# Merge stage of a two-block network on one core: gated sums by halves of the tokens, low parts on VectorE, last tile by halves of the columns

## Chip, cores and metric

One core of a Trainium2 chip runs the whole program. The metric is the device time of one execution in microseconds (us); a time is the median of several runs. The engines are named as in the profile: PE (TensorE, with PEld for its weight loads), DVE (VectorE), ACT (ScalarE), POOL (GpSimd) and SP (SyncE, which here only issues DMAs).

## What is computed

The program computes two blocks over 1024 tokens of 1024 features: a convolution mixer with a mixture of experts, then a block with sparse attention beside a state-space scan. The change touches the last lines of the second block alone:

```python
g_att, g_ssm = jnp.split(gate_logits, 2, axis=-1)
merged = jax.nn.sigmoid(g_att) * y_att + jax.nn.sigmoid(g_ssm) * y_ssm
x = x + gate[:, None, :] * (merged @ w_out[l])
```

`merged` and `x` are 1024 x 1024, `w_out` is 1024 x 1024, `gate` is one row of 1024.

## The kernel before

The last stage is `merge_out_stage`. What it reads: `k.y_ssm` (the scan's branch, in SBUF, features on the partitions, 8 chunks of 128 features x 1024 tokens, complete when the stage begins), and in DRAM `gates_dram`, whose chunks 0 to 7 hold sigmoid(g_att) * y_att (called att) and whose chunks 8 to 15 hold sigmoid(g_ssm) (called sig), `w_out_2` (the weights) and `x_dram`.

The product is made of float16 pairs: each float32 operand is split into a high part (rounded to float16) and a low part (what is left, in float16), and `product` (lines 140 to 142) issues three matmuls of 128 x 128 by 512 for every 512 columns: high by high, high by low, low by high. Weights are split by `high_part` on ACT (line 407) and `low_part` on DVE (line 412).

The stage has two phases. In the chunk loop over c = 0 to 7 (KC = 8), SP loads three tiles of 512 KB for each chunk, in the order weights, sig, att, each into a ring of four buffers (lines 2839, 2842, 2845). For c of 4 and more each load waits until its buffer is free: weights for `low`, sig for `summed`, att for `m_low`. The order of the work on each engine:

- DVE: the low part of weights 0; then for each c the product sig * y_ssm (line 2902), the sum with att (line 2905), and the low part of the weights of c + 1.
- ACT: the copy of the gate out of PSUM (line 2886); then for each c the high part of the weights (line 407) and the high part of the sums (line 2891).
- POOL: for each c the low part of the sums (line 2919).
- PE: for each c, when the four parts are there, the matmuls of the token tiles 0 to 3 (four tiles x two column halves x three), accumulated in the four PSUM tiles `mg_ps` of 1024 columns, two banks each.

In the second phase PE makes the token tiles 4 to 7, all eight chunks for each tile, 48 matmuls. For each of the eight tiles DVE multiplies the PSUM tile by the gate (line 2913), POOL adds the result to x (line 2924), and SP stores the tile of 512 KB (line 2849). x (4 MB) is loaded behind the last load of the chunk loop (line 2846). A PSUM tile is used again when its product with the gate is done (`gated_done`), a buffer of `gated` (two of them) when POOL's add is done (`added`).

All orders are written out by hand; an engine runs its list in order, and semaphores named above join the lists. What stands ahead of the stage on the engines is the scan's last projection; its last DVE instruction starts at 2716.70 us.

## Time and profile before

| | us |
|---|---|
| median of 3 runs | 2838.12 (2835.35 to 2838.47) |
| the profiled execution, its own time | 2832.92 |
| its span | 2831.1 |
| PE busy | 2513.3 (89%) |
| DVE busy | 1654.6 (58%) |
| ACT busy | 953.8 (34%) |
| POOL busy | 621.5 (22%) |
| the merge stage: first load issued, end of the span | 2718.42, 2831.1 |

The whole profile's shares are averages over stages with different limits; the merge stage is 4% of the span, and it is read by the views of its own stretch. In a row, times in a timeline are the start and the duration in us; a duration in a group of rows is the mean in ns; the last field of a row is the idle time of the engine just before it, with the instruction that ended it. PEclk is the granted clock of TensorE, 1.00 for 2.4 GHz and 0.50 for 1.2 GHz.

### The profile page before, as it was taken

What the parts mean: (1) busy time and instruction counts of PE and PEld (TensorE: products, weight loads), DVE (VectorE), ACT (ScalarE), POOL (GpSimd) and SP (SyncE); (2) the same over time, 40 slices, a digit from 0 to 9 for tenths busy, and PEclk for the clock granted to TensorE, in tenths of its full rate; (3) what the DMA queues carried; (4) which work ended last, traced back from release to release, by engine and by line L of the source; (5) the groups of instructions that cost most, each with busy time, mean ns of one, the idle gap of its engine ahead of it and who ended that gap; (6) DMA issues with size and microseconds to landing.
All of it is one profiled execution on the core that took longest, in us unless ns stands there. A gap on an engine that the chain in (4) does not pass through costs nothing. (4 is left out here: it accounts for less than half of the span.)

```text
span 2831.1 us, 39742 instructions
## 1 busy us (share of the span) xinstructions
PE 2513.3 (89%) x15455; PEld 1351.1 (48%) x15455; DVE 1654.6 (58%) x2909; ACT 953.8 (34%) x1486; POOL 621.5 (22%) x513
## 2 busy tenths in 40 slices
PE   5999594698889998589799979998999999999978
PEld 3555343354445554245334447743454444444433
DVE  5777785332223332576399986643684766746842
ACT  6110503121112222555452225531453534615510
POOL 1012123000000000332342200000450721703613
PEclk8999797799999999799899989999999999999999
DMA  9554878499999998320112210043002002020051
GB/s 240 191 167 132 286 247 318 165 384 388 386 386 372 380 366 316 100 67 23 39 37 82 104 38 1 1 149 127 16 1 97 8 1 97 8 90 8 1 218 80
DMA packets 129230, 433.06 MB, mean 153 GB/s; under 512 B 27760, under 2 KB 37360, under 8 KB 120752
## 3 DMA queue, kind: packets, MB, share of 16 engines
q1 hardware_dynamic: 99872, 365.39, 35.3%
q0 software_dynamic: 10176, 32.78, 3.7%
q10 hardware_dynamic: 19024, 32.67, 3.4%
q8 instruction: 113, 1.85, 0.3%
q14 instruction: 45, 0.37, 0.0%
HBM read 371.86 MB, written 58.94 MB: 152 GB/s over the span
## 5 line engine op out<-in xcount | busy, mean ns | idle before, releaser
L1254 PE MATMUL m_gu<-conv_y,m_xT 128*64 128x256 f32 x1024 | 234.1, 388 | 18.6 <-DMA arena<-in_moe_w_up 16.3
L1256 PE MATMUL m_gu<-arena,m_xT 128*64 128x256 f32 x1024 | 234.1, 388 | 0.0
L2307 POOL TENSOR_TENSOR group_words<-group_words 128x1024 f16<-128x1024 f16 x64 | 149.8, 2361 | 373.7 <-PE i_pj L142 364.5
L1333 DVE TENSOR_TENSOR m_hid<-m_sg,m_gu 64x256 f32<-64x256 f32 x96 | 39.6, 412 | 320.4 <-ACT m_sg L1302 320.4
L1256 PEld LDWEIGHTS m_gu<-arena,m_xT 128*64 128x64 f32 x1024 | 143.3, 140 | 73.9 <-issue 15.4
L1276 PE MATMUL m_y_ps<-arena,m_hidT 128*64 128x512 f32 x768 | 175.4, 598 | 0.0
L1302 ACT ACT_TABLE_LOAD x48 | 61.6, 1283 | 297.5 <-issue 285.0
L1254 PEld LDWEIGHTS m_gu<-conv_y,m_xT 128*64 128x64 f32 x1024 | 143.3, 140 | 36.9 <-issue 26.1
L140 PE MATMUL i_pj<-hT,group_words 128*128 128x512 f16 x384 | 146.5, 382 | 14.7 <-DVE group_words L412 9.3
L140 PE MATMUL s_pj<-hT,arena 128*128 128x512 f16 x384 | 148.7, 387 | 0.0
L141 PE MATMUL s_pj<-hT,arena 128*128 128x512 f16 x384 | 148.5, 387 | 0.0
L142 PE MATMUL s_pj<-hT,arena 128*128 128x512 f16 x384 | 148.1, 386 | 0.0
L141 PE MATMUL i_pj<-hT,group_words 128*128 128x512 f16 x384 | 146.4, 381 | 0.0
L142 PE MATMUL i_pj<-hT,group_words 128*128 128x512 f16 x384 | 146.3, 381 | 0.0
L1226 POOL COPY m_idx<-slot_token 64x1 uint32 (+1 forms) x49 | 8.7, 177 | 537.1 <-PE m_xt L1245 507.8
L1254 PE MATMUL m_gu<-hT,m_xT 128*64 128x256 f32 x512 | 114.7, 383 | 8.5 <-DMA hT<-in_moe_w_up 8.5
L1256 PE MATMUL m_gu<-hT,m_xT 128*64 128x256 f32 x512 | 114.7, 383 | 0.0
L1985 DVE TENSOR_SCALAR_CACHE_REDUCE arena<-arena,s_cand 128x384 bf16<-128x384 f32 (+1 forms) x124 | 112.3, 943 | 1.1
L1324 DVE TENSOR_SCALAR m_xT<-m_xt,row_gain 128x64 f32<-128x64 f32 x392 | 102.8, 331 | 10.5 <-PE m_xt L1245 10.5
L140 PE MATMUL q_mm<-arena,hT 128*128 128x512 f16 (+1 forms) x256 | 94.9, 371 | 7.9 <-issue 7.9
L1338 DVE TENSOR_TENSOR m_y<-m_y_ps,gate_half 128x512 f32<-128x512 f32 x48 | 33.2, 692 | 112.9 <-PE m_y_ps L1276 65.0
L141 PE MATMUL q_mm<-arena,hT 128*128 128x512 f16 (+1 forms) x256 | 94.7, 370 | 0.0
(524 smaller groups left out, 6356.8 us busy)
## 6 DMA issues: line engine op xcount, KB each, us to landing
arena<-in_moe_w_down SPq DMA_DIRECT2D x32, 2048.0 KB, 25.3
arena<-in_moe_w_up SPq DMA_DIRECT2D x22, 2048.0 KB, 23.8
conv_y<-in_moe_w_gate SPq DMA_DIRECT2D x22, 2048.0 KB, 18.1
hT<-in_moe_w_gate SPq DMA_DIRECT2D x10, 2048.0 KB, 19.0
hT<-in_moe_w_up SPq DMA_DIRECT2D x10, 2048.0 KB, 24.0
conv_y<-in_ada_w SPq DMA_DIRECT2D x8, 2048.0 KB, 8.0
x_tok<-in_ada_w ACTq DMA_DIRECT2D x6, 2048.0 KB, 12.6
slot_out<-m_y ACTq DMA_DIRECT2D x96, 128.0 KB, 8.2
```

The source lines that it names most:

```text
L140: nc.tensor.matmul(out, lhsT=lh, rhs=rh, start=start, stop=False)
L141: nc.tensor.matmul(out, lhsT=lh, rhs=rl, start=False, stop=False)
L142: return nc.tensor.matmul(out, lhsT=ll, rhs=rh, start=False, stop=stop)
L1254: g = nc.tensor.matmul(gu_ps[i][g_rows, 0:FFN // 2], lhsT=xT[:, c, :], rhs=k.wg[e % WEIGHT_SLOTS][:, c, cols], start=c == 0, stop=c == KC - 1)
L1256: u = nc.tensor.matmul(gu_ps[i][u_rows, 0:FFN // 2], lhsT=xT[:, c, :], rhs=k.wu[e % WEIGHT_SLOTS][:, c, cols], start=c == 0, stop=c == KC - 1)
L1276: last = nc.tensor.matmul(y_ps[half * BLOCK:(half + 1) * BLOCK, :], lhsT=hidT[:, c, :], rhs=k.wd[e % WEIGHT_SLOTS][:, c, half * HALF:(half ...
L1302: nc.scalar.activation(sg[:, i, :], gu_ps[i][g_rows, 0:FFN // 2], ACT.Silu).then_inc(sg_done, 1)
L1324: last = nc.vector.tensor_scalar(xT[:, c, :], xt_ps[:, c, :], gain[:, c:c + 1], shift[:, c:c + 1], ALU.mult, ALU.add)
L1333: nc.vector.tensor_tensor(hid[:, i, :], sg[:, i, :], gu_ps[i][u_rows, 0:FFN // 2], ALU.mult) \
L1338: nc.vector.tensor_tensor(y[:, :], y_ps[:, :], k.gate_half[:, :], ALU.mult).then_inc(y_read, 1)
L1985: v.tensor_scalar(junk[i % 4][:, 0:P * (blocks[i] + 1)], scores(i), threshold(i), 0.0, op, ALU.add, accum_out=count[:, i:i + 1]).then_inc( ...
L2307: return tuple(k.nc.gpsimd.tensor_tensor(k.y_U[:, t % 2, n], k.adt_parts[:, n, t, heads].unsqueeze(2).to_broadcast([P, HPG, P]), k.upto16. ...
```

## The change

- DVE works on halves of 512 tokens: product and sum of half 0, product and sum of half 1, for each chunk. The low part of the sums, in halves too, moves from POOL to DVE: the order for c of 1 and more is product, sum, product, sum, low part of half 0, low part of the weights of c + 1, low part of half 1. In chunk 0 the low part of weights 0 and that of the sums' half 0 come right after the first sum, ahead of half 1.
- ACT makes the high part of the sums in halves, with the high part of the next chunk's weights between them. The high part of weights 0 comes ahead of the copy of the gate.
- PE starts a chunk when the parts of half 0 (tokens 0 to 511, token tiles 0 to 3) are there; the parts of half 1 are waited for once, ahead of token tile 4.
- POOL has no work in the chunk loop. It still adds the token tiles 0 to 6.
- Token tile 7 is made by halves of its columns: all eight chunks of columns 0 to 511, then of 512 to 1023. DVE multiplies each half by the gate and adds it to x, and SP stores each half (256 KB).
- SP's waits for `summed` and `m_low` count both halves; the order of its loads is as before.

```diff
@@ -2823,7 +2823,8 @@
         gate_ps = acc[3]
         sig_in, att_in = ([k.sem(f"mg_{n}_in{i}") for i in range(4)] for n in ("sig", "att"))
         w_in = [k.sem(f"mg_w_in{c}") for c in range(KC)]
-        x_in, stored = k.sem("mg_x_in"), k.sem("mg_stored")
+        x_in, stored, last_added = k.sem("mg_x_in"), k.sem("mg_stored"), k.sem("mg_last_added")
+        cols = lambda h: slice(h * HALF, (h + 1) * HALF)
         high, low, mul, summed, m_high, m_low = (k.sem(f"mg_{n}") for n in (
             "high", "low", "mul", "summed", "m_high", "m_low"))
         gate_mm, gate_sb, mm_done, gated_done, added = (k.sem(f"mg_{n}") for n in (
@@ -2838,16 +2839,19 @@
                     sp.wait_ge(low, c - 3)
                 sp.dma_start(w[:, c % 4, :], ins["w_out_2"][c * P:(c + 1) * P, :]).then_inc(w_in[c], 16)
                 if c >= 4:
-                    sp.wait_ge(summed, c - 3)
+                    sp.wait_ge(summed, 2 * (c - 3))
                 sp.dma_start(sig[:, c % 4], k.gates_dram[KC + c]).then_inc(sig_in[c % 4], 16)
                 if c >= 4:
-                    sp.wait_ge(m_low, c - 3)
+                    sp.wait_ge(m_low, 2 * (c - 3))
                 sp.dma_start(att[:, c % 4], k.gates_dram[c]).then_inc(att_in[c % 4], 16)
             sp.dma_start(x, k.x_dram.rearrange("(t p) d -> p t d", p=P)).then_inc(x_in, 16)
-            for t in range(TT):
+            for t in range(TT - 1):
                 sp.wait_ge(added, t + 1)
                 sp.dma_start(out_dram[t * P:(t + 1) * P, :], x[:, t, :]).then_inc(stored, 16)
-            sp.wait_ge(stored, 16 * TT)
+            for h in range(2):
+                sp.wait_ge(last_added, h + 1)
+                sp.dma_start(out_dram[(TT - 1) * P:TT * P, cols(h)], x[:, TT - 1, cols(h)]).then_inc(stored, 16)
+            sp.wait_ge(stored, 16 * (TT + 1))
 
         @block.tensor
         def _(pe):
@@ -2857,38 +2861,50 @@
                                         rhs=k.const("ident"), start=True, stop=True)
             last.then_inc(gate_mm, 1)
 
-            def products(t, c):
-                for h in range(2):
-                    last = product(nc, acc[t % 4][:, h * HALF:(h + 1) * HALF],
-                                   part(merged, c, slice(t * P, (t + 1) * P)),
-                                   part(ws, c, slice(h * HALF, (h + 1) * HALF)), c == 0, c == KC - 1)
+            def products(t, c, halves=range(2)):
+                for h in halves:
+                    last = product(nc, acc[t % 4][:, cols(h)], part(merged, c, slice(t * P, (t + 1) * P)),
+                                   part(ws, c, cols(h)), c == 0, c == KC - 1)
                 return last
 
             pe.wait_ge(gate_sb, 1)
             for c in range(KC):
                 pe.wait_ge(high, c + 1)
                 pe.wait_ge(low, c + 1)
-                pe.wait_ge(m_high, c + 1)
-                pe.wait_ge(m_low, c + 1)
+                pe.wait_ge(m_high, 2 * c + 1)
+                pe.wait_ge(m_low, 2 * c + 1)
                 for t in range(4):
                     last = products(t, c)
                     if c == KC - 1:
                         last.then_inc(mm_done, 1)
-            for t in range(4, TT):
+            pe.wait_ge(m_high, 2 * KC)
+            pe.wait_ge(m_low, 2 * KC)
+            for t in range(4, TT - 1):
                 pe.wait_ge(gated_done, t - 3)
                 for c in range(KC):
                     last = products(t, c)
                 last.then_inc(mm_done, 1)
+            pe.wait_ge(gated_done, TT - 4)
+            for h in range(2):
+                for c in range(KC):
+                    last = products(TT - 1, c, (h,))
+                last.then_inc(mm_done, 1)
 
         @block.scalar
         def _(act):
+            def weight_high(c):
+                act.wait_ge(w_in[c], 16)
+                high_part(nc, ws[:, 0, c, :], w[:, c % 4, :]).then_inc(high, 1)
+
+            weight_high(0)
             act.wait_ge(gate_mm, 1)
             nc.scalar.activation(gate[:, :], gate_ps[:, :], ACT.Copy, scale=1.0 / W_UP).then_inc(gate_sb, 1)
             for c in range(KC):
-                act.wait_ge(w_in[c], 16)
-                high_part(nc, ws[:, 0, c, :], w[:, c % 4, :]).then_inc(high, 1)
-                act.wait_ge(summed, c + 1)
-                nc.scalar.copy(merged[:, 0, c, :], att[:, c % 4]).then_inc(m_high, 1)
+                for h in range(2):
+                    act.wait_ge(summed, 2 * c + h + 1)
+                    nc.scalar.copy(merged[:, 0, c, cols(h)], att[:, c % 4, cols(h)]).then_inc(m_high, 1)
+                    if h == 0 and c + 1 < KC:
+                        weight_high(c + 1)
 
         @block.vector
         def _(dve):
@@ -2896,30 +2912,48 @@
                 dve.wait_ge(high, c + 1)
                 low_part(nc, ws[:, 1, c, :], w[:, c % 4, :], ws[:, 0, c, :]).then_inc(low, 1)
 
-            split(0)
+            def merged_low(c, h):
+                dve.wait_ge(m_high, 2 * c + h + 1)
+                nc.vector.tensor_tensor(merged[:, 1, c, cols(h)], att[:, c % 4, cols(h)], merged[:, 0, c, cols(h)],
+                                        ALU.subtract).then_inc(m_low, 1)
+
             for c in range(KC):
-                dve.wait_ge(sig_in[c % 4], 16 * (c // 4 + 1))
-                nc.vector.tensor_tensor(sig[:, c % 4], sig[:, c % 4], k.y_ssm[:, c, :], ALU.mult).then_inc(mul, 1)
-                dve.wait_ge(mul, c + 1)
-                dve.wait_ge(att_in[c % 4], 16 * (c // 4 + 1))
-                nc.vector.tensor_tensor(att[:, c % 4], att[:, c % 4], sig[:, c % 4], ALU.add).then_inc(summed, 1)
+                for h in range(2):
+                    s, a = sig[:, c % 4, cols(h)], att[:, c % 4, cols(h)]
+                    dve.wait_ge(sig_in[c % 4], 16 * (c // 4 + 1))
+                    nc.vector.tensor_tensor(s, s, k.y_ssm[:, c, cols(h)], ALU.mult).then_inc(mul, 1)
+                    dve.wait_ge(mul, 2 * c + h + 1)
+                    dve.wait_ge(att_in[c % 4], 16 * (c // 4 + 1))
+                    nc.vector.tensor_tensor(a, a, s, ALU.add).then_inc(summed, 1)
+                    if c == h == 0:
+                        split(0)
+                        merged_low(0, 0)
+                if c:
+                    merged_low(c, 0)
                 if c + 1 < KC:
                     split(c + 1)
+                merged_low(c, 1)
             dve.wait_ge(gate_sb, 1)
-            for t in range(TT):
+            for t in range(TT - 1):
                 dve.wait_ge(mm_done, t + 1)
                 if t >= 2:
                     dve.wait_ge(added, t - 1)
                 nc.vector.tensor_tensor(gated[:, t % 2], acc[t % 4][:, :], gate[:, :], ALU.mult).then_inc(gated_done, 1)
+            dve.wait_ge(added, TT - 2)
+            dve.wait_ge(x_in, 16)
+            for h in range(2):
+                dve.wait_ge(mm_done, TT + h)
+                part_of = gated[:, (TT - 1) % 2, cols(h)]
+                nc.vector.tensor_tensor(part_of, acc[(TT - 1) % 4][:, cols(h)], gate[:, cols(h)], ALU.mult) \
+                    .then_inc(gated_done, 1)
+                dve.wait_ge(gated_done, TT + h)
+                nc.vector.tensor_tensor(x[:, TT - 1, cols(h)], x[:, TT - 1, cols(h)], part_of, ALU.add) \
+                    .then_inc(last_added, 1)
 
         @block.gpsimd
         def _(pool):
-            for c in range(KC):
-                pool.wait_ge(m_high, c + 1)
-                nc.gpsimd.tensor_tensor(merged[:, 1, c, :], att[:, c % 4], merged[:, 0, c, :], ALU.subtract) \
-                    .then_inc(m_low, 1)
             pool.wait_ge(x_in, 16)
-            for t in range(TT):
+            for t in range(TT - 1):
                 pool.wait_ge(gated_done, t + 1)
                 nc.gpsimd.tensor_tensor(x[:, t, :], x[:, t, :], gated[:, t % 2], ALU.add).then_inc(added, 1)
 
```

## Rows read from the trace of the kernel before

**Rows 1.** The chain that ended last, one period of the chunk loop: start us, us, what.

```profile
2739.20 1.24 DVE mg_att L2905
...
2742.53 2.18 issue
...
2745.95 1.24 DVE mg_att L2905
```

**Rows 2.** Windows: us, busy (x instructions) of PE, PEld, DVE, ACT, POOL, PEclk, DMA, GB/s.

```profile
2722.00:2726.00 4.00, 0.00 (x0) 0.00 (x0) 2.68 (x3) 1.06 (x1) 0.00 (x0) 0.79 1.00 389
2726.00:2734.00 8.00, 3.67 (x9) 1.31 (x10) 5.55 (x4) 2.31 (x3) 2.12 (x1) 0.50 1.02 414
...
2738.00:2777.60 39.60, 31.63 (x143) 13.43 (x142) 25.63 (x18) 11.06 (x11) 12.74 (x6) 1.00 0.62 238
2777.60:2824.40 46.80, 46.78 (x216) 21.03 (x216) 8.57 (x7) 0.00 (x0) 16.32 (x7) 1.00 0.20 79
```

**Rows 3.** Groups by line and shape, 2715 to 2832: busy us, mean ns, idle before.

```profile
L140 PE MATMUL mg_ps<-mg_ws,mg_merged 128*128 128x512 f16 x128 | 49.4, 386 | 17.8 <-POOL mg_merged L2919 17.8
```

**Rows 4.** Timeline of PE: start us, us, instruction, idle before and its releaser.

```profile
2730.33 0.59 PE L140 MATMUL mg_ps<-mg_ws,mg_merged 128*128 128x512 f16 x1 [9.84 <-POOL mg_merged L2919]
...
2737.59 0.38 PE L140 MATMUL mg_ps<-mg_ws,mg_merged 128*128 128x512 f16 x1
...
2777.61 0.38 PE L140 MATMUL mg_ps<-mg_ws,mg_merged 128*128 128x512 f16 x1 [1.41 <-POOL mg_merged L2919]
...
2824.01 0.38 PE L142 MATMUL mg_ps<-mg_ws,mg_merged 128*128 128x512 f16 x1
```

**Rows 5.** DMA issues, KB, us to landing: two single issues (rows 8), then whole span.

```profile
mg_att<-gate_tiles SPq DMA_DIRECT2D x1, 512.0 KB, 5.4
...
mg_w<-in_w_out SPq DMA_DIRECT2D x1, 512.0 KB, 12.0
...
hT<-x_second SPq DMA_DIRECT2D x1, 4096.0 KB, 13.8
out_x<-hT SPq DMA_DIRECT2D x8, 512.0 KB, 2.6
...
conv_y_phases<-cy_sb SPq DMA_DIRECT2D x1, 256.0 KB, 2.0
```

**Rows 6.** Timeline of the end: the last instructions of DVE and POOL.

```profile
2824.43 1.23 DVE L2913 TENSOR_TENSOR mg_gated<-mg_ps,mg_gate 128x1024 f32<-128x1024 f32 x1 [9.14 <-PE mg_ps L142]
...
2825.73 2.34 POOL L2924 TENSOR_TENSOR hT<-hT,mg_gated 128x1024 f32<-128x1024 f32 x1 [8.01 <-DVE mg_gated L2913]
```

**Rows 7.** Timeline, ACT's first weights, then DVE's first chunk and the next low half.

```profile
2722.20 1.06 ACT L407 ACTIVATE mg_ws<-mg_w 128x1024 f16<-128x1024 f32 x1 [0.65 <-DMA mg_w<-in_w_out]
...
2723.28 1.23 DVE L412 SCALAR_TENSOR_TENSOR mg_ws<-mg_w,mg_ws 128x1024 f16<-128x1024 f32 x1 [5.90 <-ACT mg_ws L407]
2724.43 1.22 DVE L2902 TENSOR_TENSOR mg_sig<-mg_sig,y_ssm 128x1024 f32<-128x1024 f32 x1
2725.68 1.22 DVE L2905 TENSOR_TENSOR mg_att<-mg_att,mg_sig 128x1024 f32<-128x1024 f32 x1
2728.97 2.29 DVE L412 SCALAR_TENSOR_TENSOR mg_ws<-mg_w,mg_ws 128x1024 f16<-128x1024 f32 x1 [2.07 <-ACT mg_ws L407]
```

**Rows 8.** Timeline, the first low half on POOL, and two issues of SP's queue.

```profile
2728.06 2.12 POOL L2919 TENSOR_TENSOR mg_merged<-mg_att,mg_merged 128x1024 f16<-128x1024 f32 x1 [57.43 <-ACT mg_merged L2891]
...
2719.27 0.42 SPq L2845 DMA_DIRECT2D mg_att<-gate_tiles  x1
...
2723.07 0.43 SPq L2839 DMA_DIRECT2D mg_w<-in_w_out  x1
```

**Rows 9.** Groups of the whole span, instructions of 512 elements on DVE and ACT.

```profile
L2789 DVE TENSOR_TENSOR z_ssm<-z_ssm,group_words 128x512 f32<-128x512 f32 x32 | 22.1, 692 | 1.1
...
L2801 DVE TENSOR_TENSOR yT<-y_tr,yT 128x512 f16<-128x512 f32 x32 | 21.8, 682 | 1.4 <-ACT yT L2725 1.4
...
L782 ACT CAST hT<-conv_y 128x512 f16<-128x512 f32 x8 | 4.8, 601 | 0.0
```

## Prediction

> **What bounds the kernel now.** I read the chain of waits first, since the change touches one stage alone, the merge, which is the last 113 us of the span of 2831.1 us. In its chunk loop the chain repeats with a period of 6.75 us: sum on DVE, then ACT's high half of the sums, then ACT's high half of the next weights, then 2.18 us shown as issue, which is DVE's low half of the weights, then DVE's product and sum of the next chunk [rows 1]. TensorE is not in it. A chunk is 24 matmuls; 216 of them in 46.8 us make 0.216 us from start to start [rows 2], so 5.18 us, and the grouped view has TensorE idle for 17.8 us before the merge's matmuls, waiting for GpSimd's low half of the sums [rows 3]: 9.84 us before the first chunk [rows 4], none before the second, and (17.8 - 9.84) / 6 = 1.33 on average before each of the other six. From 2777.61, where the 8th chunk starts, TensorE is busy without a hole to 2824.4 [rows 2, 4]: the 8th chunk (5.18) and four token tiles of 48 matmuls (10.36 each). So the stage is bound by the DVE-ACT chain up to 2777.6, by TensorE up to 2824.4, and by a serial tail: DVE 1.23, GpSimd 2.34, store 2.6 [rows 5, 6].
>
> The DVE rows of the first chunk show what the loop is made of. The first low half of weights takes 1.23 us, the next 2.29 [rows 7]. The second overlaps GpSimd's 2.12 us instruction (2728.06 to 2730.18), and it ends 1.08 us behind that [rows 7, 8]. The change empties GpSimd in the loop, so I take 1.23 for every one.
>
> **The change, part by part.** I rebuild the schedule step by step. Prices: a DVE instruction of 1024 elements takes 1.22, the next starts 1.15 after its start when it waits for nothing fresh, 1.25 when it reads its result [rows 7]. One of 512 elements takes 0.69, with both inputs in SBUF, with a 16-bit output or from PSUM [rows 9]; by the same overlap and gap its steps are 0.62 and 0.72. ACT's copy of 512 takes 0.60 [rows 9], its high half of weights 1.06 [rows 7]; I take steps of 0.55 and 0.95, DVE's overlap and a little more.
>
> *Start.* The weights of chunk 0 land at 2722.2 [rows 7], att at 2719.27 + 5.4 = 2724.67 [rows 5, 8], and sig, which lies between them in the queue, one load of 512 KB ahead of att, which at 410 GB/s is 1.28 us: about 2723.4. The new DVE order is product half at 2723.4, sum half at 2724.70 (att ends that wait), weights' low half 2725.32 to 2726.55, sums' low half 2726.47 to 2727.16. ACT's high half of the sums (2725.42 to 2726.0) hides beside the weights' low half. With the 0.15 us that TensorE took after its releaser (2728.06 + 2.12 = 2730.18 to 2730.33) [rows 4, 8] it starts at 2727.3, not 2730.33: 3.0 us earlier. ACT's gate copy now queues behind the wait for the weights (2722.2) and ends near 2724.2 instead of 2721.55; its reader TensorE starts later anyway, so this costs nothing.
>
> *First chunk.* TensorE's granted clock is 0.79 in 2722 to 2726 and 0.50 in 2726 to 2734 [rows 2], so it fell to 1.2 GHz while it stood idle. The first chunk took 2737.59 - 2730.33 = 7.26 us [rows 4]: 2.08 more than 5.18, ten matmuls at twice 0.216, so it rose to 2.4 GHz some 4 us after the matmuls began. The new idle time is 6.8 us instead of 9.8, still beyond the place where the clock fell, so I take 7.26 again. Bound: 5.18 if it stays up, and then chunk 1 waits for DVE.
>
> *Second chunk ready.* From 2727.09 DVE does a product and a sum half (0.72, 0.62), low half of weights 1 (1.15), low half of the sums (0.62), then of chunk 1 product, sum, product, sum (0.72, 0.62, 0.72, 0.62) and its first low half (0.69): 2733.57. TensorE wants it at 2727.3 + 7.26 = 2734.56, so it doesn't wait. Were the clock up all along, chunk 1 would start at 2733.7, 0.8 us better; that is the low bound.
>
> *Loop.* DVE per chunk: 0.72 + 0.62 + 0.72 + 0.62 + 0.62 + 1.15 + 0.62 = 5.07 us. ACT: 0.55 + 0.95 + 0.55, and the weights' high part is done 0.2 us before DVE wants it (sum half ready at +1.41 of the chunk, then 0.60 and 1.05 with overlap gives +3.1; DVE's low half of weights is due at +3.3). Behind ACT's wait for the next weights now stands the second high half. Those weights are early: chunk 3's, the tightest, land at 2723.07 + 12.0 = 2735.1 and ACT wants them near 2737.3 [rows 5, 8]. So DVE at 5.07 stays ahead of TensorE at 5.18, and TensorE sets the period; the upper bound is 5.57 for DVE, if each half takes 0.69 plus the 0.03 gap and the weights' low half 1.25.
>
> *Loads.* SP now waits for both halves of sums and low parts; its order of issue is kept. A chunk is three loads of 512 KB, 1.57 MB; at the 410 GB/s or so of the full stretch [rows 2] that is 3.8 us against 5.18. Chunk 7's last load is issued near 2745.5 and lands near 2753, and is wanted at 2760.6. The 4 MB load of x behind it took 13.8 us [rows 5]; it ends near 2763, and GpSimd first wants it near 2768. If it came 8 us later still nothing would move, since TensorE needs the third gated tile only two token tiles (20.7 us) later.
>
> *Sum for the loop.* Chunk 7 starts at 2734.56 + 6 x 5.18 = 2765.6, against 2777.61: 12.0 us gained, the start among it. The wait for the second token half falls under chunk 7's own 5.18 us. From there to TensorE's end the matmuls are the same number in another order: nothing gained.
>
> *Tail.* Now, from TensorE's end at 2824.4 to the span's end it is 6.7 us [rows 4, 6]. Afterwards the first column half is multiplied, added and stored under the second half's 5.18 us of matmuls; behind the last matmul stand 0.03 + 0.69 + 0.06 + 0.69 + 0.02, then a store of 256 KB. The nearest row is the one 256 KB store of the trace, 2.0 us against 2.6 for 512 KB [rows 5]; then 0.4 as now. That is 3.9 us: 2.8 gained; 2.2 if the store doesn't shrink, and as much upward, 3.4, for the other end. DVE's wait for GpSimd's sixth sum is long over then; the cover, were it gone, would cost at most that instruction's 2.35.
>
> Two rules of the Trainium skill are weighed here. The page SBUF — State Buffer, section Who interferes with whom, states that a VectorE instruction with two SBUF inputs and a GpSimd instruction that reads SBUF block each other for a whole instruction; by it the 2.29 holds 1.06 of blocking, which goes when GpSimd is empty, and if the rule were not at work here rival (b) would be the sum. Against cutting in halves speaks the page VectorE: DVE Perf Modes, section The TRN2 errata: the fixed cost is paid by every instruction, so small tiles pay it more often. By its formula three more instructions in a chunk cost 3 x 151 / 0.96 = 472 ns, an estimate; the rows' 0.692 against half of 1.22 give three times 0.08, on each half, the same 0.49, which stands in the 5.07.
>
> **The forecast.** 12.0 + 2.8 = 14.8 us. The profiled execution goes from 2831.1 to 2816.3 of span (its own time was 2832.92, 1.8 above its span). The median of the runs, 2838.12, stands 5.2 above the profiled execution; taking the same offset, 2838.1 - 14.8 = 2823.3 us.
>
> **Rivals.**
>
> (a) *DVE sets the period.* Each half at its full duration: 5.57 per chunk. Chunk 1 would be ready at 7.0 instead of 6.4 after TensorE's start, so before the clock-slowed first chunk ends, and the loop loses 6 x 0.39 = 2.3 us: 2825.6. For it: the margin is only 0.11 us per chunk. Against: the step of 1.15 without a fresh wait [rows 7].
>
> (b) *DVE's low part of weights stays at 2.29*, because its cause is the loads and not GpSimd. DVE then needs 6.13 per chunk, chunk 1 is ready at 7.4, and the loop loses some 6 us: 2829.3. Against: the first one took 1.23 with the DMA share already 1.00 [rows 2, 7].
>
> (c) *The change doesn't shorten the loop*: the period stays 6.75 by a wait between ACT and DVE that I have not seen; 3.0 of start and 2.8 of tail are left, 2832.3.
>
> (d) *Slower*: TensorE's clock doesn't rise after the first chunk. A matmul then takes 0.43 instead of 0.216 as in the first chunk; the gain of 14.8 is used up after 14.8 / 0.216 = 69 more slow matmuls, three chunks, and if it held for the remaining 360 the time would be 2823.3 + 78 = 2901. Against: in the loop now the clock is 1.00 in spite of a hole of 1.3 us in each chunk [rows 2], and the new loop has fewer holes. The Trainium skill (TensorE: Matmul & The Clock Gate, Seeing it yourself) reports gates seen stuck low; no row here shows one.
>
> **How the numbers follow.** Forecast 0.75, (a) 0.12, (b) 0.05, (c) 0.03, (d) 0.02, other 0.03. Low end: 2823.3 less 0.8 (clock), 0.5 (tail) and 2.8 (how far the lowest run lies below the median) = 2819. High end: (b), 2829.5, which takes in (a). A measurement of this kernel can tell about 0.2%, 5.7 us. Faster by more: forecast, (a), (b) and part of the rest, 0.93; within: (c) and a mishap, 0.04; slower 0.03.
>
> **What would show it.** The low half of weights at 1.22 to 1.23 in every chunk; TensorE's idle time before the merge's matmuls near 7 us in all, nearly all of it before the first; the first matmul 3 us earlier after the first load; chunk 7 about 38 us after it; period 5.18; behind the last matmul 3.9 us. Wrong: DVE periods over 5.2 with TensorE waiting for DVE's low half (a, b), ACT waiting for a load, or a granted clock under 1.00 after the first chunk (d).

## The result, and the profile after

The changed kernel takes 2821.74 us in the median of 6 runs (2819.21 to 2824.51), the kernel before 2838.18 beside it: a ratio of 0.9945, 95% interval 0.9933 to 0.9957. Two later sets of five runs gave 0.9955 (0.9942 to 0.9969) and 0.995 (0.9936 to 0.9963). The forecast was 2823.3, faster by 14.8 us; the medians differ by 16.4, in the two later sets by 13.6 and 14.3.

The profiled execution has a span of 2820.3 us. The stage itself is measured from the first load's issue to the span's end: 2831.1 - 2718.42 = 112.7 us before, 2820.3 - 2721.31 = 99.0 after, 13.7 us less. What stands ahead of the stage was the same work and took 2.9 us longer in this execution, so the stage and not the span is what is compared below.

The groups by line and shape of the changed kernel, 2710 to 2822, which answer to [rows 3]:

```profile
L140 PE MATMUL mg_ps<-mg_ws,mg_merged 128*128 128x512 f16 x128 | 49.4, 386 | 8.0 <-DVE mg_merged L2917 8.0
...
L412 DVE SCALAR_TENSOR_TENSOR mg_ws<-mg_w,mg_ws 128x1024 f16<-128x1024 f32 x8 | 9.8, 1219 | 0.0
```

The windows of the same trace, columns as in [rows 2]:

```profile
2726.00:2730.00 4.00, 0.00 (x0) 0.00 (x0) 1.88 (x3) 2.43 (x3) 0.00 (x0) 0.83 0.95 342
2730.00:2734.00 4.00, 2.61 (x7) 0.96 (x8) 3.96 (x6) 1.77 (x3) 0.00 (x0) 0.50 1.02 401
2734.00:2738.00 4.00, 4.00 (x17) 1.64 (x16) 3.93 (x7) 2.09 (x3) 0.00 (x0) 0.81 1.02 415
2738.00:2765.00 27.00, 27.00 (x127) 12.23 (x126) 26.62 (x39) 10.43 (x15) 0.00 (x0) 1.00 1.01 403
2765.00:2816.40 51.40, 51.40 (x239) 23.10 (x237) 13.17 (x14) 1.24 (x2) 16.32 (x7) 1.00 0.20 78
```

TensorE now waits once, 8.0 us ahead of the first chunk, and for DVE; from there its busy time equals the window (27.00 of 27.00, 51.40 of 51.40). DVE is busy 26.62 of 27.00 us in the chunk loop, so it has become the next bound. The clock shows the same hole as before: 0.83, then 0.50, then 0.81, and 1.00 from 2738 on. The weights' low half has a mean of 1219 ns over all eight, at a DMA share of 1.01.

The DVE timeline of the start and of one later chunk, which answers to [rows 7]:

```profile
2727.50 0.69 DVE L2924 TENSOR_TENSOR mg_sig<-mg_sig,y_ssm 128x512 f32<-128x512 f32 x1 [7.23 <-DMA mg_sig<-gate_tiles]
2728.82 0.69 DVE L2927 TENSOR_TENSOR mg_att<-mg_att,mg_sig 128x512 f32<-128x512 f32 x1 [0.62 <-DMA mg_att<-gate_tiles]
2729.43 1.22 DVE L412 SCALAR_TENSOR_TENSOR mg_ws<-mg_w,mg_ws 128x1024 f16<-128x1024 f32 x1
2730.56 0.69 DVE L2917 TENSOR_TENSOR mg_merged<-mg_att,mg_merged 128x512 f16<-128x512 f32 x1
...
2739.23 0.69 DVE L2924 TENSOR_TENSOR mg_sig<-mg_sig,y_ssm 128x512 f32<-128x512 f32 x1
2739.95 0.69 DVE L2927 TENSOR_TENSOR mg_att<-mg_att,mg_sig 128x512 f32<-128x512 f32 x1
2740.56 0.68 DVE L2924 TENSOR_TENSOR mg_sig<-mg_sig,y_ssm 128x512 f32<-128x512 f32 x1
2741.28 0.69 DVE L2927 TENSOR_TENSOR mg_att<-mg_att,mg_sig 128x512 f32<-128x512 f32 x1
2741.88 0.68 DVE L2917 TENSOR_TENSOR mg_merged<-mg_att,mg_merged 128x512 f16<-128x512 f32 x1
2742.49 1.22 DVE L412 SCALAR_TENSOR_TENSOR mg_ws<-mg_w,mg_ws 128x1024 f16<-128x1024 f32 x1
2743.62 0.69 DVE L2917 TENSOR_TENSOR mg_merged<-mg_att,mg_merged 128x512 f16<-128x512 f32 x1
2744.22 0.68 DVE L2924 TENSOR_TENSOR mg_sig<-mg_sig,y_ssm 128x512 f32<-128x512 f32 x1
```

From 2739.23 to 2744.22 the period is 4.99 us: product, sum, product, sum, low half of the sums, low half of the weights, low half of the sums, without an idle field on any of them. At the start both first instructions wait for their loads, and TensorE's 8.0 us of idle time follow from that; the forecast had near 7.

TensorE's timeline, first and last matmul of the stage, answering to [rows 4]:

```profile
2731.39 0.59 PE L140 MATMUL mg_ps<-mg_ws,mg_merged 128*128 128x512 f16 x1 [8.02 <-DVE mg_merged L2917]
...
2816.06 0.38 PE L142 MATMUL mg_ps<-mg_ws,mg_merged 128*128 128x512 f16 x1
```

DVE's timeline, its last two instructions, answering to [rows 6]:

```profile
2816.48 0.69 DVE L2947 TENSOR_TENSOR mg_gated<-mg_ps,mg_gate 128x512 f32<-128x512 f32 x1 [3.66 <-PE mg_ps L142]
2817.20 0.69 DVE L2950 TENSOR_TENSOR hT<-hT,mg_gated 128x512 f32<-128x512 f32 x1
```

TensorE needs 85.05 us from 2731.39 to 2816.44 (a matmul's end is 0.38 behind its start). Then 0.69, 0.69 and a store: 3.86 us to the end of the span.

The timeline of SP's queue, the first, third and fourth issue, which answers to [rows 8]:

```profile
2721.31 0.33 SPq L2840 DMA_DIRECT2D mg_w<-in_w_out  x1
...
2722.16 2.22 SPq L2846 DMA_DIRECT2D mg_att<-gate_tiles  x1
2724.43 0.43 SPq L2840 DMA_DIRECT2D mg_w<-in_w_out  x1
```

The third issue takes 2.22 us where it took 0.42. The loads of this execution landed late: weights 0 at 4.9 us after the first issue, att 0 at 7.4, against 3.8 and 6.2 in the kernel before.

### The profile page after: what moved, and what is told of

It reads as the page before. It is cut to its first block and busy times, and to the rows that moved or that the text cites. A ratio compares the mean times of both kernels' runs of the same rounds, so it can differ in the third digit from the quotient of the medians.

```text
span 2820.3 us, 39786 instructions
## 1 busy us (share of the span) xinstructions
PE 2518.0 (89%) x15455; PEld 1353.6 (48%) x15455; DVE 1660.1 (59%) x2944; ACT 955.1 (34%) x1494; POOL 603.4 (21%) x504
## 5 line engine op out<-in xcount | busy, mean ns | idle before, releaser
L140 PE MATMUL i_pj<-hT,group_words 128*128 128x512 f16 x384 | 146.3, 381 | 14.8 <-DVE group_words L412 9.4
L140 PE MATMUL q_mm<-arena,hT 128*128 128x512 f16 (+1 forms) x256 | 94.3, 368 | 7.9 <-issue 7.9
L1302 ACT ACTIVATE m_sg<-m_gu 64x256 f32<-64x256 f32 x96 | 36.6, 382 | 170.8 <-PE m_gu L1254 100.2
```

The source lines that it names most:

```text
L140: nc.tensor.matmul(out, lhsT=lh, rhs=rh, start=start, stop=False)
L1302: nc.scalar.activation(sg[:, i, :], gu_ps[i][g_rows, 0:FFN // 2], ACT.Silu).then_inc(sg_done, 1)
```

## The experiments

Twelve further runs were made, two of them of the changed kernel itself; each was profiled once and timed in 5 to 11 executions beside the kernel before, which has a single profile of its own. The three durations that make up the stage are read from each profile's timelines: from the first load's issue to the first matmul of the chunk loop (start), from there to TensorE's end (TensorE), and from there to the span's end (tail). "w0, att0" are the landings of chunk 0's weights and of its att, counted from the first issue.

| kernel | ratio to before (95%) | w0, att0 | start | TensorE | tail | stage |
|---|---|---|---|---|---|---|
| before | 1 | 3.8, 6.2 | 11.91 | 94.06 | 6.71 | 112.7 |
| changed | 0.9945 (0.9933-0.9957) | 4.9, 7.4 | 10.08 | 85.05 | 3.86 | 99.0 |
| changed, second set | 0.9955 (0.9942-0.9969) | 5.2, 7.7 | 10.39 | 84.71 | 3.93 | 99.0 |
| changed, third set | 0.995 (0.9936-0.9963) | 3.6, 8.3 | 10.96 | 85.60 | 3.85 | 100.4 |
| tail alone | 0.9989 (0.998-0.9998) | 5.3, 7.9 | 13.49 | 94.07 | 3.87 | 111.4 |
| loop alone | 0.996 (0.9947-0.9974) | 3.7, 8.6 | 11.32 | 84.46 | 6.74 | 102.5 |
| whole tokens | 0.9963 (0.9949-0.9976) | 3.6, 7.9 | 12.89 | 85.36 | 3.92 | 102.2 |
| ACT's other order | 0.9967 (0.9954-0.9979) | 3.5, 8.0 | 10.65 | 91.58 | 3.90 | 106.1 |
| low halves on GpSimd | 0.9963 (0.9949-0.9977) | 5.3, 7.9 | 10.91 | 88.09 | 3.95 | 103.0 |
| three tiles in the loop | 0.9974 (0.9962-0.9985) | 5.1, 7.6 | 10.28 | 92.13 | 3.92 | 106.3 |
| hole filled | 0.995 (0.9937-0.9964) | 3.5, 8.2 | 10.89 | 84.19 | 3.90 | 99.0 |
| lagged halves, hole filled | 0.9952 (0.9938-0.9965) | 4.9, 7.5 | 10.14 | 86.80 | 3.87 | 100.8 |
| the same, first loads halved | 0.9948 (0.9934-0.9961) | 3.6, 7.4 | 10.11 | 86.73 | 3.87 | 100.7 |
| lagged halves, mended | 0.9936 (0.9922-0.9949) | 3.8, 7.9 | 10.57 | 83.04 | 3.90 | 97.5 |

The medians tell differences of some 4 us; the parts of the stage repeat within 0.1 us in the tail and within 1.2 us in TensorE's part, so what is said below rests on the parts. Of TensorE's part it is the first chunk that differs: it took 6.6 to 7.7 us in the five profiles in which TensorE has no hole behind its start and none was filled, with 7 to 12 matmuls at the lower clock. A difference of 1 us or less is therefore read as an effect only where the rows show its place.

**The theory and its rivals.** Theory: the chunk loop was held by a ring of DVE and ACT with GpSimd's instruction blocking one of DVE's; the change leaves DVE 5.0 us of work for a chunk and asks ACT for nothing at the last moment, so TensorE's 5.18 sets the period; the tail is a serial chain that got shorter. Rivals: that the halves themselves, or ACT's place for the weights' high part, or the emptied GpSimd alone are what counts, and that DVE sets the new period. The last one is tested under Three tiles in the loop.

### The tail alone

```diff
-            for t in range(4, TT):
+            for t in range(4, TT - 1):
...
+            for h in range(2):
+                for c in range(KC):
+                    last = products(TT - 1, c, (h,))
+                last.then_inc(mm_done, 1)
```

(on the kernel before, with the DVE, GpSimd and SP sides of the last tile as in the change)

> The kernel before with the last token tile alone changed: column halves, its two sums on DVE, two stores of 256 KB. Theory (the three parts of the gain add up; the tail is a serial chain behind the last matmul): from TensorE's last end to the span's end 3.85 us instead of 6.7, the chunk loop as before (TensorE idle 17.8 us before the stage's matmuls), median 2838.2 - 2.85 = 2835.3 us. Rival (the end of the span is set by something other than this chain): tail still near 6.7, 2838 us.

The tail is 3.87 instead of 6.71, 2.84 us less, and TensorE's part stays at 94.07. The ratio 0.9989 is 3.1 us, its interval 0.6 to 5.7. The groups of this kernel, 2720 to 2834, still show the old loop:

```profile
L140 PE MATMUL mg_ps<-mg_ws,mg_merged 128*128 128x512 f16 x128 | 49.4, 386 | 19.5 <-POOL mg_merged L2937 19.5
```

The start took 13.49 us with the same code that took 11.91 in the kernel before; in both the first matmul stands 8.1 to 8.2 us behind the landing of the first weights. This kernel's landings (5.3 and 7.9) are nearly those of the changed kernel's second profile (5.2 and 7.7), whose start is 10.39. At equal landings the new order thus starts 3.1 us earlier, where the first pair of profiles shows 1.8.

### The loop alone

```diff
-            for t in range(4, TT - 1):
+            for t in range(4, TT):
...
-                    last = products(TT - 1, c, (h,))
```

(on the changed kernel, DVE, GpSimd and SP alike)

> The changed kernel with the last tile as before (whole, sum on GpSimd, one store). Theory: TensorE busy without a hole from its first matmul of the chunk loop to its end, 85 us, tail 6.7 us; 2821.7 + 2.85 = 2824.6 us. Rival (the last tile's halves also cost TensorE or GpSimd something that this takes back): 2823 or less.

TensorE's part 84.46, tail 6.74. The two parts are independent: 94.06 - 84.46 = 9.6 from the loop and 2.84 from the tail, each as large alone as together within what repeats. The start differs for a reason of its own, which the DVE timeline of this kernel shows, first two instructions:

```profile
2728.13 0.69 DVE L2916 TENSOR_TENSOR mg_sig<-mg_sig,y_ssm 128x512 f32<-128x512 f32 x1 [7.18 <-DMA mg_sig<-gate_tiles]
2730.72 0.69 DVE L2919 TENSOR_TENSOR mg_att<-mg_att,mg_sig 128x512 f32<-128x512 f32 x1 [1.90 <-DMA mg_att<-gate_tiles]
```

The second one, the first sum, waited 1.90 us more for att 0, which landed 8.6 us after the first issue. TensorE began 2.7 us after that landing, as in every run of the changed order (10.08 - 7.4, 10.39 - 7.7, 10.96 - 8.3).

### The changed kernel again, twice

> The changed kernel itself, beside the others. 2821.7 us. What the profile should settle is the start of the stage: in the first profile TensorE began the chunk loop 10.1 us after the first load was issued, where 8.9 was forecast, with one issue of SP at 2.2 us instead of 0.4. Theory (a chance of that execution): 8.9 to 9.5 us here and issues of 0.4. Rival (the changed order or the place of the instructions makes SP slow): 10 us again, with the long issue at the same place.

> The changed kernel itself, beside the next three. 2822.4 us; TensorE starts the chunk loop 10 to 11 us after the first load is issued and then needs 85.0 us; the sum's weights of the start: att lands 7.4 to 8.6 us after that issue (it was 6.2 in the profile of the kernel before, the only one of nine), and the first matmul follows 2.7 us later.

A long issue on SP (1.3 to 2.4 us) is there in every profile but that of the kernel before, whatever the order, as the second to the fifth issue; in the three profiles of the changed kernel it is the third, the fifth and the second. It is neither of the two things that I had put against each other: not a chance of one execution, and not of the changed order either, since the tail alone has it too. Where it is the second issue, that of sig 0, weights 0 land early (3.5 to 3.8) and att 0 late (7.9 to 8.6, and 7.4 where that load is halved); where it comes later, the two landings lie 2.5 us apart. What makes it long was not tried, nor whether a second profile of the kernel before would have one.

### Whole tokens

```diff
-                for h in range(2):
-                    act.wait_ge(summed, 2 * c + h + 1)
-                    nc.scalar.copy(merged[:, 0, c, cols(h)], att[:, c % 4, cols(h)]).then_inc(m_high, 1)
-                    if h == 0 and c + 1 < KC:
-                        weight_high(c + 1)
+                if c + 1 < KC:
+                    weight_high(c + 1)
+                act.wait_ge(summed, c + 1)
+                nc.scalar.copy(merged[:, 0, c, :], att[:, c % 4]).then_inc(m_high, 1)
```

(DVE: product, sum, low half of the weights of c + 1, low half of the sums, each in one instruction of 1024)

> The changed kernel without halves of the tokens in the chunk loop: low half of the sums on DVE in one instruction of 1024, ACT makes the next weights' high half ahead of the sums' high half. Theory (what freed the loop is that no engine waits for ACT between the steps and that GpSimd is empty; the halves only bring the first matmul forward): DVE per chunk 1.25 + 1.15 + 1.15 + 1.15 = 4.7 us, TensorE without holes at 5.18, first matmul some 2 us later, 2823.7 us. Rival (the halves are what hides ACT's work): TensorE waits in every chunk, 1 us or more each, 2829 us or more.

The DVE timeline of this kernel, one chunk and the start of the next:

```profile
2739.62 1.22 DVE L2915 TENSOR_TENSOR mg_sig<-mg_sig,y_ssm 128x1024 f32<-128x1024 f32 x1
2740.87 1.22 DVE L2918 TENSOR_TENSOR mg_att<-mg_att,mg_sig 128x1024 f32<-128x1024 f32 x1
2742.01 1.22 DVE L412 SCALAR_TENSOR_TENSOR mg_ws<-mg_w,mg_ws 128x1024 f16<-128x1024 f32 x1
2743.21 1.23 DVE L2922 TENSOR_TENSOR mg_merged<-mg_att,mg_merged 128x1024 f16<-128x1024 f32 x1
2744.35 1.22 DVE L2915 TENSOR_TENSOR mg_sig<-mg_sig,y_ssm 128x1024 f32<-128x1024 f32 x1
```

DVE's period is 2744.35 - 2739.62 = 4.73 us, TensorE's part 85.36 without a hole. So the halves are not what freed the loop: without them DVE has 0.26 us more room for each chunk. They bring the first matmul forward: 12.89 - 7.9 = 5.0 us behind att 0's landing here, 2.7 with halves, 2.3 us off the stage. The rival falls. What this kernel doesn't separate is ACT's order from the low half of the sums on DVE, since it has both. An estimate from the rows of the kernel before: with GpSimd empty and ACT's order kept, the ring of 6.75 us loses 2.29 - 1.22 = 1.07 and stays at some 5.7, over TensorE's 5.18. Whether ACT's order alone would have been enough for whole tokens was not tried; with halves the next two kernels take each of the two back.

### ACT's other order

```diff
-                    if h == 0 and c + 1 < KC:
-                        weight_high(c + 1)
+                if c + 1 < KC:
+                    weight_high(c + 1)
```

> The changed kernel with the high half of the next weights behind both high halves of the sums on ACT, not between them. Theory: DVE's low half of the weights, due 3.3 us into the chunk, must wait for ACT until about 4.3, so DVE's period is 6.05 us instead of 5.0 and TensorE idles about 0.9 us before each of six chunks: 5.4 us slower, 2827.1 us. Rival (the order on ACT doesn't matter since ACT is 40% busy): no idle time of TensorE, 2821.7 us.

Timelines of this kernel, two DVE instructions of a chunk and TensorE's first matmul of the next:

```profile
2739.55 0.68 DVE L2917 TENSOR_TENSOR mg_merged<-mg_att,mg_merged 128x512 f16<-128x512 f32 x1
2741.27 1.23 DVE L412 SCALAR_TENSOR_TENSOR mg_ws<-mg_w,mg_ws 128x1024 f16<-128x1024 f32 x1 [1.04 <-ACT mg_ws L407]
...
2746.50 0.38 PE L140 MATMUL mg_ps<-mg_ws,mg_merged 128*128 128x512 f16 x1 [0.78 <-DVE mg_merged L2917]
```

DVE's low half of the weights waits 1.04 us for ACT in each chunk, the period is 6.12 instead of 5.18, and TensorE stands idle 0.78 to 1.00 us before each of seven chunks (counted from the modelled end of the matmul before, 0.38 behind its start): TensorE's part 91.58, 6.5 us more where 5.4 were expected. ACT works 0.62 + 0.62 + 1.05 = 2.3 us in a period of 6.12, and its order still costs 6.5 us; with halves the place of the weights' high part between them is needed.

### The low halves of the sums on GpSimd

```diff
+            for c in range(KC):
+                for h in range(2):
+                    pool.wait_ge(m_high, 2 * c + h + 1)
+                    nc.gpsimd.tensor_tensor(merged[:, 1, c, cols(h)], att[:, c % 4, cols(h)],
+                                            merged[:, 0, c, cols(h)], ALU.subtract).then_inc(m_low, 1)
```

(and DVE's `merged_low` taken out)

> The changed kernel with the low halves of the sums on GpSimd again, two instructions of 512 for each chunk. Theory (GpSimd's instruction and DVE's with two SBUF inputs exclude each other): DVE instructions that overlap them are stretched up to 1.15 us, the period of DVE is between 5.0 and 6.1 instead of 5.0 in spite of 1.24 us less work on it; first matmul 0.5 us later; 2822.5 to 2827 us. Rival (the 2.29 us of the kernel before came from something else): every DVE instruction keeps 0.69 and 1.22, DVE needs 3.8 per chunk, TensorE sets the period, 2822.2 us.

Timelines of this kernel, DVE over a period (the weights' low half, the two instructions behind it, the next low half), then the second of GpSimd's two of that chunk, and GpSimd's sixteen in the tile's view (shortest, median and longest in ns):

```profile
2740.15 1.78 DVE L412 SCALAR_TENSOR_TENSOR mg_ws<-mg_w,mg_ws 128x1024 f16<-128x1024 f32 x1 [0.32 <-ACT mg_ws L407]
2741.85 1.64 DVE L2919 TENSOR_TENSOR mg_sig<-mg_sig,y_ssm 128x512 f32<-128x512 f32 x1
2743.52 0.69 DVE L2922 TENSOR_TENSOR mg_att<-mg_att,mg_sig 128x512 f32<-128x512 f32 x1
...
2745.86 1.78 DVE L412 SCALAR_TENSOR_TENSOR mg_ws<-mg_w,mg_ws 128x1024 f16<-128x1024 f32 x1 [0.32 <-ACT mg_ws L407]
...
2740.81 2.13 POOL L2949 TENSOR_TENSOR mg_merged<-mg_att,mg_merged 128x512 f16<-128x512 f32 x1
...
L2949 POOL TENSOR_TENSOR mg_merged<-mg_att,mg_merged x16: 1154/1616/2137, 2732.4 to 2775.1; 128x512 f16<-128x512 f32 x16
```

DVE has two instructions less in a chunk, and its period is 2745.86 - 2740.15 = 5.71 us, over TensorE's 5.18. The two instructions that start while GpSimd is at work are stretched, 1.22 to 1.78 and 0.69 to 1.64; one that starts just ahead of GpSimd's (2739.14) or beside an empty GpSimd keeps 0.69. GpSimd's own two take 1.61 and 2.13, in a row from 2739.23 to 2742.94; the shortest of the sixteen, 1.15 us, is the very last, behind DVE's last instruction of the loop. DVE's 1.78 ends 1.09 us behind GpSimd's first, GpSimd's second ends 1.01 behind that, and DVE's 1.64 ends 0.55 behind it: each a little less than its time alone (1.22, 1.15, 0.69). The two engines hold up each other in turn. This is what the page SBUF — State Buffer of the Trainium skill, section Who interferes with whom, says of two SBUF inputs beside a GpSimd instruction that reads SBUF. TensorE's part is 88.09, some 3 us more than in the changed kernel. The run also decides rival (b) of the prediction, along with the mean of 1219 ns at a DMA share of 1.01 shown above: the loads have no part in it.

### Three tiles in the loop

```diff
-                for t in range(4):
+                for t in range(3):
                     last = products(t, c)
...
-            for t in range(4, TT - 1):
-                pe.wait_ge(gated_done, t - 3)
+            for t in range(3, TT - 1):
+                if t >= 4:
+                    pe.wait_ge(gated_done, t - 3)
```

> The changed kernel with three token tiles in the chunk loop and five behind it, the same matmuls in all. TensorE's share of a chunk falls from 5.18 to 3.89 us, so DVE must show as the bound. Theory: period 5.0 us (DVE's own), TensorE idle 1.1 us before each chunk but the second, some 6.6 us slower, 2828.3 us: the margin of DVE below TensorE is 0.18 us for each chunk. Rival (a load or ACT stands right behind TensorE): a period over 5.1, with DVE waiting.

TensorE's timeline of this kernel, the first matmul of two chunks in a row:

```profile
2742.27 0.38 PE L140 MATMUL mg_ps<-mg_ws,mg_merged 128*128 128x512 f16 x1 [0.95 <-DVE mg_merged L2918]
...
2747.26 0.38 PE L140 MATMUL mg_ps<-mg_ws,mg_merged 128*128 128x512 f16 x1 [0.95 <-DVE mg_merged L2918]
```

With 3.89 us of matmuls in a chunk the period is 4.99 and TensorE waits 0.95 for DVE each time; TensorE's part grows by 7.1 us (6.6 expected). So DVE stands right behind TensorE, 0.19 us for each chunk, as computed, and rival (a), a DVE period of 5.57, is out.

### The hole filled

```diff
             last.then_inc(gate_mm, 1)
+            for i in range(28):
+                nc.tensor.matmul(acc[0][:, 0:P], lhsT=k.const("ident"), rhs=k.const("ident"), start=True, stop=True)
```

> The changed kernel with 28 matmuls of 128 x 128 by 128 more on TensorE, behind those of the gate; their result is written over. They fill 7 us of the hole ahead of the chunk loop. Theory (the first chunk is slow because the clock fell in that hole, and behind it DVE's second chunk stands 6.3 us after TensorE's start): granted clock 1.00 throughout, the first chunk takes 5.18 us, then a wait of 1.1 us for DVE, TensorE needs 84.2 us instead of 85.0: 2821.6 us, 0.8 less than the kernel itself. Rival (the clock falls all the same, or the first chunk is slow for another reason): 7.2 us for the first chunk again.

TensorE's timeline of this kernel, the fillers, then the first matmuls of chunks 0 and 1:

```profile
2722.72 6.42 PE L2864 MATMUL mg_ps<-consts 128*128 128x128 f32 x56
2731.71 0.38 PE L140 MATMUL mg_ps<-mg_ws,mg_merged 128*128 128x512 f16 x1 [2.58 <-DVE mg_merged L2919]
...
2738.04 0.38 PE L140 MATMUL mg_ps<-mg_ws,mg_merged 128*128 128x512 f16 x1 [0.98 <-DVE mg_merged L2919]
```

The fillers (28 matmuls of float32, shown as 56 instructions) take 6.42 us and leave holes of 2.58 and, before chunk 1, of 0.98 us. The granted clock stayed at 1.00, the first chunk took its 5.18 us, and chunk 1 waited for DVE as forecast: it starts 2738.04 - 2731.71 = 6.33 us after TensorE did. TensorE's part is 84.19; against 84.71 to 85.60 that is 0.5 to 1.4 us. The medians (2823.38 and 2824.29) can't tell it.

### Lagged halves, and the first loads halved

```diff
+        order = [(0, 0)] + [p for c in range(1, KC) for p in ((c, 0), (c - 1, 1))] + [(KC - 1, 1)]
```

(DVE and ACT go through this order, on DVE with product, sum, for half 0 the weights' low half, then the low half of the sums)

> The kernel with the 28 matmuls, and the second token half of each chunk put behind the first half of the next one, on DVE and ACT alike (its parts are wanted only by token tile 4). Theory: DVE has the second chunk ready 3.3 us after TensorE's start and each further one 5.0 later, so that nothing holds TensorE: 83.1 us from its start to its end, 2820.5 us, 1.9 less than the kernel itself. Rival (the loads are late for this order): TensorE or DVE waits for a load in chunk 1 to 3.

> The kernel of the run before with 24 matmuls instead of 28, and sig and att of chunk 0 loaded by halves of 256 KB, the second halves behind the loads of chunk 1. Theory: att's first half lands 1.3 us earlier, TensorE starts 9.0 us after the first issue instead of 10.3, then 83.1 us as in the run before: 2819.2 us, 3.2 less than the kernel itself. Rival (small loads cost more, or the second halves come too late): start unchanged, or DVE waits for them.

Both missed: TensorE's part is 86.80 and 86.73, not 83.1. The DVE timeline of the first one, product, sum and low half of a second half, shows why:

```profile
2739.00 0.69 DVE L2921 TENSOR_TENSOR mg_sig<-mg_sig,y_ssm 128x512 f32<-128x512 f32 x1
2739.72 0.69 DVE L2924 TENSOR_TENSOR mg_att<-mg_att,mg_sig 128x512 f32<-128x512 f32 x1
2741.09 0.69 DVE L2928 TENSOR_TENSOR mg_merged<-mg_att,mg_merged 128x512 f16<-128x512 f32 x1 [0.68 <-ACT mg_merged L2908]
```

For a second half nothing stands between the sum and its low half, so DVE waits 0.68 us for ACT's copy; the period is 5.77. I had counted DVE's work and not its wait. Chunk 7 starts 38.65 us behind the first matmul, where 7 x 5.18 = 36.3 were possible: 2.4 us. The rest of the loss comes right behind the chunk loop. DVE multiplies token tile 0 by the gate only after the last second halves, at 2773.26, and TensorE waits for that before token tile 4 (timeline of TensorE, the first kernel):

```profile
2774.62 0.38 PE L140 MATMUL mg_ps<-mg_ws,mg_merged 128*128 128x512 f16 x1 [1.20 <-DVE mg_gated L2935]
```

The second kernel's start was 10.11 us, not 9.0: att's first half landed at 7.4. In it the clock fell although the fillers had left a hole of only 2.68 us, where a hole of 2.58 us in the kernel above didn't let it fall. The granted clock was still 1.00 in the hole and for the first 0.4 us of matmuls, and 0.50 from 2733.2 to 2736 (windows of the second kernel, up to the chunk loop, its first 0.4 and its first 3.6 us; PEclk is the third number from the end):

```profile
2730.00:2732.40 2.40, 0.00 (x1) 0.03 (x1) 2.25 (x3) 1.62 (x2) 0.00 (x0) 1.00 1.02 405
2732.40:2732.80 0.40, 0.40 (x2) 0.19 (x3) 0.40 (x1) 0.00 (x0) 0.00 (x0) 1.00 1.06 415
2732.40:2736.00 3.60, 3.60 (x10) 1.35 (x11) 2.91 (x4) 0.62 (x1) 0.00 (x0) 0.58 1.04 420
```

This cost TensorE's part nothing (86.73 beside 86.80), since DVE's longer period set it.

### Lagged halves, mended

```diff
+                gated_sum(c, 0)
+                if c:
+                    gated_sum(c - 1, 1)
+                split(c)
+                merged_low(c, 0)
+                if c:
+                    merged_low(c - 1, 1)
```

> The lagged order of the token halves once more, mended: on DVE the product and sum of chunk c half 0 and of chunk c - 1 half 1 come first, then the low half of the weights, then both low halves of the sums, so that DVE never asks ACT for what it has just handed over; 34 matmuls fill the hole ahead of the chunk loop, loads as in the changed kernel. Theory (in the lagged order before, each low half right behind its own sum waited 0.68 us for ACT, which made DVE's period 5.77 and cost TensorE what the clock had given back): no wait of DVE for ACT, period 5.0, second chunk ready 4.5 us after TensorE's start, granted clock 1.00, TensorE 83.1 us from start to end against 84.7 to 85.6 in the changed kernel. The median would be 1.9 us below the changed kernel's, about 0.07%, which the medians can hardly tell. Rival (something else in the lagged order stretches the loop): TensorE over 84 us with waits in the middle of the loop.

The DVE timeline of this kernel: the product that opens a period, the weights' low half, both low halves of the sums together, the next product:

```profile
2749.88 0.69 DVE L2926 TENSOR_TENSOR mg_sig<-mg_sig,y_ssm 128x512 f32<-128x512 f32 x1
...
2752.54 1.22 DVE L412 SCALAR_TENSOR_TENSOR mg_ws<-mg_w,mg_ws 128x1024 f16<-128x1024 f32 x1
2753.67 1.29 DVE L2920 TENSOR_TENSOR mg_merged<-mg_att,mg_merged 128x512 f16<-128x512 f32 x2
2754.88 0.69 DVE L2926 TENSOR_TENSOR mg_sig<-mg_sig,y_ssm 128x512 f32<-128x512 f32 x1
```

The instructions left out have no idle field either. The period is 5.00, and TensorE's part is 83.04 us, which is 384 matmuls at 0.216 without any hole or slow one (82.9). With the hole filled in the changed kernel's order it was 84.19. The 34 fillers of this kernel left a hole of 0.91 us. The stage takes 97.5 us, 1.5 less than the changed kernel's best. Its median is 2819.59 us beside 2836.77, a ratio of 0.9936 (0.9922 to 0.9949): it beats the kernel before clearly; against the changed kernel's 0.9945, 0.9955 and 0.995 the gain is in the stage's parts, and the intervals overlap.

## Why the prediction was right, point by point

**The sum.** Forecast 12.0 for start and loop and 2.8 for the tail. Of the 12.0, start was 3.0 and TensorE's part 9.0 (94.1 to 85.1). Measured in the profiles: TensorE's part 94.06 to 85.05, 9.0 (9.35 and 8.5 with the 84.71 and 85.60 of the two others, so the exact match of the first is luck); tail 6.71 to 3.86, 2.85, also with the last tile changed alone. These two were right in size and cause.

**The first chunk.** It was taken at 7.26 us again, since the clock would have fallen within 6.8 us of idle time. The clock fell, and the first chunk took 7.19, 6.85 and 7.73 us in the three profiles of the changed kernel, 6.59 with the loop alone; that is the 1.1 us by which TensorE's part differs where it has no hole (84.46 to 85.60). The kernel with the hole filled shows what it costs: with the clock up it is DVE that decides chunk 1, at 6.33 us after the start against 6.4 forecast.

**The loop.** DVE's period was computed as 5.07 and is 4.99; each term held: 0.61 and 0.72 as steps (0.62 and 0.72 taken), 1.13 for the weights' low half (1.15 taken). The weights' low half lasts 1.22 us in every chunk, as forecast for an empty GpSimd. The three more instructions of the halves cost DVE 4.99 - 4.73 = 0.26 us a chunk, where the prediction put 0.49: their durations grow by that, but the steps overlap. No engine waits for a load after those of chunk 0. Chunk 7 was forecast some 38 us after the first matmul; 7.19 + 6 x 5.18 = 38.3, without a hole. The forecast said that TensorE sets the period with a margin of 0.11 and that the rest is hidden; the kernel with three tiles measured 0.19.

**The start, the one term that was off.** 3.0 us were forecast; the first pair of profiles gives 11.91 - 10.08 = 1.8. The step that failed is the landing of the first loads, taken from one execution: att 0 at 6.2 us after the first issue. In every other profile it landed at 7.4 to 8.6. The same delay made TensorE's idle time 8.0 us instead of 6.8. What I worked out behind it holds: 2.6 us from att's landing to the first matmul in the forecast, 2.7 measured. In the old order the first matmul comes 8.1 to 8.2 us behind the landing of weights 0, in the new one 2.7 behind that of att 0; so at a distance of 2.5 us between the two landings the start gains 5.45 - 2.5 = 3.0, which the kernel with the tail alone bears out (3.1 at equal landings, both late). Where att 0 comes more than 3.5 us behind the weights, the old order's sum would have to wait for it too, and about 2 us would be left: an estimate, the 4.65 us from that sum to the first matmul in the kernel before (2725.68 to 2730.33) less the 2.65 of the new order. No kernel of the old order had such landings. At equal landings the parts give 9.0 + 2.85 + 3.1 = 15.0 us, and the medians of the three sets 16.4, 13.6 and 14.3; the three ratios with their intervals are 8.8 to 19.0 us. So 14.8 is not contradicted, nor is it confirmed to a microsecond, and the closeness of 2821.7 to 2823.3 owes something to chance.

**The rivals.** (a) is out by the measured period of 4.99. The high end of the range was given as (b) at 2829.5, and (b) itself as 2829.3; nothing hangs on the 0.2. (b) is out by 1219 ns at full DMA share and by the low halves on GpSimd. (c) would have shown TensorE waiting in each chunk; ACT's other order is what that looks like (TensorE's part 91.58), and it is one line away. (d): the granted clock of the changed kernel is 1.00 from 2738 to TensorE's end.

## What to carry to other kernels

Before counting what an edit takes off an engine, list the ring that sets the period, and for each step what it was handed just before: an engine that is busy for 2.3 of 6.1 us cost 6.5 us by its order alone, and a low half right behind its own sum cost 0.68 us in each chunk. Moving work from GpSimd to DVE was a gain of 3 us though DVE was the busier of the two, because instructions with two SBUF inputs on both sides at once stretched both. Cut into halves what stands between the first load and the first matmul; a loop bound elsewhere gains nothing from it.

## What the runs showed of the hardware that I had not expected

- A DVE instruction with two SBUF inputs and a GpSimd one that reads SBUF hold up each other, not DVE alone: GpSimd's instruction of 512 elements took 1.61 and 2.13 us beside DVE's and 1.15 with DVE idle, and DVE's went from 0.69 to 1.64.
- The first loads of this stage landed at times that differ by 1.8 us (weights 0, 3.5 to 5.3) and 2.4 us (att 0, 6.2 to 8.6) from profile to profile with the same order of issue, with one issue of 1.3 to 2.4 us among the first five in 13 of 14 profiles. The cause stays open.
- TensorE's clock fell to 0.50 some 0.5 us behind a hole of 2.68 us in one run, and stayed at 1.00 over a hole of 2.58 us in another, as over the holes of 0.8 to 1.4 us in the loops.
